# Six projection groups of a decoder step multiplied in plain fp32 from raw weights, with their norm scaling on VectorE

## The chip, the cores and the metric

The kernel runs on one NeuronCore of one Trainium2 chip. The metric is the device time of one execution in microseconds, the median of several runs. Engines are named TensorE (PE in the profile), VectorE (DVE), ScalarE (ACT), GpSimd (POOL) and SyncE (SP, which here only issues transfers).

## The reference

One layer of a decoder, for a prompt of 256 tokens and 8 decode tokens, everything in float32:

```
x = x + 0.5 * post1(SwiGLU_1(pre1(x)))
h = rms_norm(x, g_pre) @ w_in             # 2048 -> 5120: q, k, v of 8 window heads and of 4 stick-breaking heads, q of 4 memory heads
q, k of the window heads are rotated (rope)
o = [dilated window attention | stick-breaking attention | memory attention]
x = x + post(concat(rms_norm of each part of o) @ w_out)
x = x + 0.5 * post2(SwiGLU_2(pre2(x)))
```

The 264 tokens go through the dense parts together. The prompt attends to itself and to a memory of 256 rows; each decode token attends to its cache: 2048 positions of stick-breaking keys in pages of 128, the window keys and 256 memory rows. The new keys and values are outputs too.

## The kernel before

Activations lie transposed in SBUF: 16 tiles of 128 features by 264 tokens (xT). Every dense layer runs over weight **chunks** of 1 MB (4 x 128 rows by 512 columns), loaded by SyncE into four slots `raw`. A chunk is two **units**. For a unit ScalarE rounds the weights to a high half (`wh<-raw`, L780), VectorE subtracts that for the low half (`wl<-raw,wh`, L1111), and TensorE makes three products of a reduced fp32 type for each tile: high x high, high x low and low x high (L471 to L473, in `unit`). The activations have such halves too, xh and xl. The splits run three units ahead of the products (`AHEAD`), and semaphores count them: `hi_made`, `lo_made`, `unit_used`.

The input projection (L578 to L602) has ten groups of 512 columns, each four chunks. Groups 0 to 3 give the queries: VectorE takes them from PSUM with the norm factor r_pre (`take_projection`). Groups 4 to 9 give keys and values: ScalarE copies them into kv (`take_kv`, L896), GpSimd makes the low halves of their weights (L1657) and multiplies kv by r_pre (`scale_kv`, L1664).

While groups 5 to 9 run, VectorE goes through the decode **sequences** (`sequence`, L1295, two hardware loops of four with the rotation of the new keys between them). A sequence has 12 key tiles: 8 of paged keys, 3 of window keys, 1 of memory keys. For each tile VectorE makes 8 dot products of the keys with the query rows (L1305, k_cache). SyncE's queue holds the order of the loads (L409 to L423): for each sequence its query rows, its 12 key tiles into four slots, each as the slot is freed (`k_used`), and behind every fourth tile the next weight chunk. k_cache lies over xT, which is parked in DRAM for that time.

The queries must first leave TensorE: after group 4 it turns them (L597), ScalarE copies them (q_s, L912), GpSimd stores them to q_scratch, and SyncE loads them back onto all partitions (q_rows, L388).

When all 24 tiles of kv are scaled (`kv_scaled`), TensorE turns them into 18 rows of 512 (L615, L617). ScalarE copies them out, twelve of them through two alternating buffers `rows` (L931) that GpSimd's stores must free, six into v_rows. In ScalarE's order the scores of the decode tokens (zt, L951) come behind these rows, and they need the whole sequence loop. Then come the values of the caches, w_out and the second feed-forward part.

## Time and profile before

| | |
|---|---|
| runs of before | 2578.55, 2571.93, 2576.32 us; median 2576.32 |
| profiled execution | span 2581.1 us; no time of its own is listed beside it |
| PE busy | 2227.8 us, 86% of the span |
| DVE, ACT, POOL busy | 1546.8, 1016.3, 484.8 us |
| transfers | 468.32 MB, mean 181 GB/s |

Stages in the span, read from the chain in order of time: memory projection and first feed-forward part to about 905 us, input projection and sequence loop to 1368, attention to about 1612, output projection and second feed-forward part to the end. Busy shares are averages over stages with different limits, so a stage is read by its own stretch. A duration of a matmul in the trace reaches over its pipeline; the distance of two starts is what it costs in a row of them.

### The profile page before, as it was taken

Reading aid. Unit: us, or ns where it says so; the run is one execution under the profiler, and the core shown is the slowest. Engines: PE = TensorE matmul, PEld = TensorE weight load, DVE = VectorE, ACT = ScalarE, POOL = GpSimd, SP = SyncE. Lnnn points to the kernel's source line nnn. Section 1 sums busy time; section 2 is a strip of 40 time slices with the busy share of each in tenths; the row PEclk is TensorE's granted clock in tenths of the full one; section 3 lists DMA queues with packets and bytes.
Section 4 is the critical chain, followed back from the end, with each engine's and each line's share of the span. In section 5 each row is a group of like instructions: output and inputs, shape, how many; then the busy total and the mean of one; then the engine's idle time right before and its main releaser. Section 6 shows DMA issues by size and latency. Waiting matters only on the chain.

```text
span 2581.1 us, 44451 instructions
## 1 busy us (share of the span) xinstructions
PE 2227.8 (86%) x16613; PEld 2104.8 (82%) x16613; DVE 1546.8 (60%) x3309; ACT 1016.3 (39%) x1300; POOL 484.8 (19%) x444
## 2 busy tenths in 40 slices
PE   6899999999999879665545766888999999999997
PEld 6899999999999869655532323878999999999996
DVE  6655555554545574588787866546554555555456
ACT  3443343443434443211125775334443334343343
POOL 4600000000000242535331212035000000000004
PEclk9999999999999989877767988888999999999998
DMA  7355455554555537577786965343554545455451
GB/s 255 122 196 180 163 180 164 180 180 164 177 167 180 164 98 244 158 249 252 224 292 221 289 209 175 131 147 115 181 181 162 181 163 180 164 180 181 163 180 66
DMA packets 230311, 468.32 MB, mean 181 GB/s; under 512 B 12689, under 2 KB 13714, under 8 KB 229346
## 3 DMA queue, kind: packets, MB, share of 16 engines
q1 hardware_dynamic: 227602, 460.78, 54.3%
q0 software_dynamic: 2528, 4.89, 0.5%
q8 instruction: 144, 2.36, 0.4%
q14 instruction: 37, 0.30, 0.0%
HBM read 456.40 MB, written 9.21 MB: 180 GB/s over the span
## 4 chain that ended last, share of the span: by engine, by line
PE 70%; DVE 14%; DMA 5%; POOL 3%; ACT 3%; issue 3%; SPq 1%; DVEq 0%; ACTq 0%; POOLq 0%
PE ps L471 23%; PE ps L472 22%; PE ps L473 22%; DVE k_cache L1305 6%; DMA k_cache<-win_k 2%; DVE vl L1469 2%; DVE wl L1111 1%; POOL acc L1589 1%; DMA k_cache<-sb_k 1%; ACT wh L780 1%; POOL wl L1657 1%; ACT vh L1019 1%; DVE y L1173 1%; PE ps L702 1%; PE ps L704 1%
## 5 line engine op out<-in xcount | busy, mean ns | idle before, releaser
L471 PE MATMUL ps<-xh,wh 128*128 128x264 f32 (+1 forms) x3840 | 1136.8, 296 | 197.0 <-POOL wl L1657 106.5
L1111 DVE TENSOR_TENSOR wl<-raw,wh 128x1024 fp32r<-128x1024 f32 x605 | 749.9, 1243 | 814.6 <-ACT wh L780 813.5
L780 ACT ACTIVATE wh<-raw 128x1024 fp32r<-128x1024 f32 x656 | 690.2, 1058 | 1277.4 <-PE ps L473 1046.8
L472 PE MATMUL ps<-xl,wh 128*128 128x264 f32 (+1 forms) x3840 | 1127.5, 294 | 0.0
L473 PE MATMUL ps<-xh,wl 128*128 128x264 f32 (+1 forms) x3840 | 1125.6, 293 | 0.0
L471 PEld LDWEIGHTS ps<-xh,wh 128*128 128x128 f32 x3840 | 761.0, 198 | 213.5 <-POOL wl L1657 98.1
L472 PEld LDWEIGHTS ps<-xl,wh 128*128 128x128 f32 x3840 | 760.6, 198 | 0.0
L473 PEld LDWEIGHTS ps<-xh,wl 128*128 128x128 f32 x3840 | 758.1, 197 | 0.0
L471 PE MATMUL ps<-hh,wh 128*128 128x264 f32 x1408 | 400.6, 284 | 0.0
L473 PE MATMUL ps<-hh,wl 128*128 128x264 f32 x1408 | 400.5, 284 | 0.0
L472 PE MATMUL ps<-hl,wh 128*128 128x264 f32 x1408 | 400.3, 284 | 0.0
L1642 POOL TENSOR_TENSOR gate<-gate,r_pre 128x264 f32<-128x264 f32 x88 | 85.5, 1001 | 1330.8 <-ACT gate L837 1330.8
L1305 DVE CUSTOM_DVE_ANT_0 k_cache<-k_cache,q_rows 128x128 f32<-128x128 f32 (+1 forms) x768 | 228.5, 365 | 73.6 <-DMA k_cache<-win_k 42.4
L471 PEld LDWEIGHTS ps<-hh,wh 128*128 128x128 f32 x1408 | 265.6, 189 | 0.0
L472 PEld LDWEIGHTS ps<-hl,wh 128*128 128x128 f32 x1408 | 265.3, 188 | 0.0
L473 PEld LDWEIGHTS ps<-hh,wl 128*128 128x128 f32 x1408 | 264.7, 188 | 0.0
L1657 POOL TENSOR_TENSOR wl<-raw,wh 128x1024 fp32r<-128x1024 f32 x51 | 129.3, 2552 | 225.9 <-ACT wh L780 225.8
L1469 DVE TENSOR_TENSOR vl<-v_cache,vh 128x1024 fp32r<-128x1024 f32 (+1 forms) x96 | 116.3, 1240 | 50.4 <-ACT vh L1019 50.0
L702 PE MATMUL ps<-vh,weights 128*8 128x512 f32 (+1 forms) x192 | 86.4, 450 | 55.7 <-DVE vl L1469 54.8
L1204 DVE TENSOR_TENSOR y<-y,ps 128x264 f32<-128x264 f32 x352 | 127.4, 423 | 5.1 <-PE ps L473 5.0
L1019 ACT ACTIVATE vh<-v_cache 128x1024 fp32r<-128x1024 f32 (+1 forms) x96 | 98.7, 1049 | 28.6 <-PE ps L704 19.2
L702 PEld LDWEIGHTS ps<-vh,weights 128*8 128x8 f32 (+1 forms) x192 | 18.0, 94 | 110.7 <-DVE vl L1469 86.0
(215 smaller groups left out, 1247.1 us busy)
## 6 DMA issues: line engine op xcount, KB each, us to landing
raw<-w_gu SPq DMA_DIRECT2D x176, 1024.0 KB, 5.0
raw<-w_down SPq DMA_DIRECT2D x88, 1024.0 KB, 5.1
raw<-w_in SPq DMA_DIRECT2D x40, 1024.0 KB, 6.3
k_cache<-sb_k SPq DMA_DIRECT2D x128, 256.0 KB
v_cache<-sb_v SPq DMA_DIRECT2D x128, 256.0 KB, 3.6
raw<-w_out SPq DMA_DIRECT2D x16, 1024.0 KB, 5.2
raw<-w_mem_kv SPq DMA_DIRECT2D x8, 1024.0 KB, 10.2
k_cache<-win_k SPq DMA_DIRECT2D x16, 384.0 KB
```

The lines of the kernel that those rows point to most:

```text
L471: pe.matmul(out, w_hi, rh(k0 + kk), start=first and kk == 0, stop=False)
L472: pe.matmul(out, w_hi, rl(k0 + kk), start=False, stop=False)
L473: mm = pe.matmul(out, w_lo, rh(k0 + kk), start=False, stop=last and kk == 1)
L702: pe.matmul(out[0:8, :], weights[0:n, 2 * k + j, b], vh[slot][0:n, part], start=first, stop=False, skip_group_check=True)
L780: act.activation(wh[:, c % UNIT_SLOTS], raw[:, raw_slot, 2 * (c % 2):2 * (c % 2) + 2], ACT.Copy).then_inc(hi_made, 1)
L1019: act.activation(vh[slot][0:n], v_cache[0:n, tile % V_SLOTS], ACT.Copy).then_inc(vh_made, 1)
L1111: dve.tensor_tensor(wl[:, c % UNIT_SLOTS], raw[:, (c // 2) % RAW_SLOTS, part], wh[:, c % UNIT_SLOTS].bitcast(F32), ALU.subtract).then_inc( ...
L1204: dve.tensor_tensor(y[:, b], y[:, b], ps[4 * (q % 2) + j][:, 0:TOK], ALU.add).then_inc(y_added[l], 1)
L1305: return dve.tensor_tensor_reduce(keys, keys, q_rows[0:n, HD * q_head:HD * q_head + HD], 1.0, 0.0, ALU.mult, ALU.add, zb[0:n, col:col + 1])
L1469: dve.tensor_tensor(vl[slot][0:n], v_cache[0:n, tile % V_SLOTS], vh[slot][0:n].bitcast(F32), ALU.subtract).then_inc(vl_made, 1)
L1642: pool.tensor_tensor(gate[:, j], gate[:, j], r_pre[:], ALU.mult).then_inc(gate_ready[l], 1)
L1657: pool.tensor_tensor(wl[:, c % UNIT_SLOTS], raw[:, (c // 2) % RAW_SLOTS, part], wh[:, c % UNIT_SLOTS].bitcast(F32), ALU.subtract).then_inc ...
```

## The change

Groups 4 to 9 are multiplied in plain fp32: one product of the raw weights with xg, the activations times the norm's gain, where there were three of the halves (`plain_chunk`). ScalarE makes xg after group 3, over xh. No weights of these groups are split, so GpSimd has no arithmetic there, and the counts that later stages wait for are lowered by `SPLIT_SKIP` = 48 units. A chunk is loaded when the products of the chunk four before it are done. The queries are turned after two chunks of group 4. VectorE scales kv (`scale_kv`) at five places in the sequence loop, which is written out, and once behind it. SyncE loads the chunks 16 to 19 ahead of the first key tiles, and these wait for xg.

```diff
+SPLIT_SKIP = 2 * (CH_OUT - CH_PLAIN)
...
+def made(unit):
+    return unit if unit < 2 * CH_PLAIN else unit - SPLIT_SKIP
...
+            xg = sb("xg", [P, KT, TOK], F32, part)
...
+                if 20 <= n < 44:
+                    sp.wait_ge(unit_used, unit_of(CH_IN + n - 3))
+                    load_chunk(CH_IN + n, c, src, first=True)
+                else:
+                    load_chunk(CH_IN + n, c, src, skip=SPLIT_SKIP if n >= 44 else 0)
...
-            for n in range(12, 16):
+            for n in range(12, 20):
                 load_in(n)
             sp.wait_ge(x_parked, 16)
+            sp.wait_ge(xg_ready, KT)
             for k in range(K_SLOTS):
                 load_tile(0, k, k_cache[:, k], k_loaded[k], sb_k, win_k, mem_k)
-            for n in range(16, 16 + 6):
+            for n in range(20, 16 + 6):
                 load_in(n)
...
+            def plain_chunk(g, c, guard=None):
+                n, bank = CH_IN + 4 * g + c, 4 * (g % 2)
+                pe.wait_ge(w_loaded[c], 16 * (n // RAW_SLOTS + 1))
+                for j in range(4):
+                    if c == 0:
+                        pe.wait_ge(in_read, (g - 2) * 4 + (j + 1))
+                    if guard is not None:
+                        guard(j)
+                    for kk in range(4):
+                        k = 4 * c + kk
+                        if g == 4 and j == 0:
+                            pe.wait_ge(xg_ready, k + 1)
+                        mm = pe.matmul(ps[bank + j][:, 0:TOK], raw[:, c, kk, P * j:P * j + P], xg[:, k],
+                                       start=k == 0, stop=k == KT - 1)
+                    if c == 3 and j < 3:
+                        mm.then_inc(in_done, 1)
+                mm.then_inc(unit_used, 2)
...
-            for c in range(8, 32):
+            for c in range(8, 32 - AHEAD):
                 split(u_in + c + AHEAD)
+            act.wait_ge(unit_used, u_in + 32)
+            for k in range(KT):
+                act.activation(xg[:, k], xT[:, k], ACT.Copy, scale=G[:, G_PREM + k:G_PREM + k + 1]
+                               ).then_inc(xg_ready, 1)
...
+            def scale_kv(g):
+                at = 4 * (g - 4)
+                for j in range(4):
+                    dve.wait_ge(in_read, 4 * g + j + 1)
+                    dve.tensor_tensor(kv[:, at + j], kv[:, at + j], r_pre[:], ALU.mult).then_inc(kv_scaled, 1)
...
+                    g, after = divmod(b * TILES_B + k + 38, 16)
+                    if after == 0 and 4 <= g < 9:
+                        scale_kv(g)
...
-            with dve.Fori(0, DEC // 2) as b:
+            for b in range(DEC // 2):
                 sequence(b)
             dve.wait_ge(kv_scaled, H_WIN)
             rope(kv[:, 0:H_WIN])
-            with dve.Fori(DEC // 2, DEC) as b:
+            for b in range(DEC // 2, DEC):
                 sequence(b)
+            scale_kv(9)
```

TensorE's order around the turning of the queries (qT), which before stands between groups 4 and 5:

```order
L473 MATMUL ps<-xh,wl 128x264
L597 MATMUL ps<-ident,qT 8x128 [waits in_read,roped]
L597 MATMUL ps<-ident,qT 8x128 x15
L471 MATMUL ps<-xh,wh 128x264 [waits q_s_made,lo_made]
L472 MATMUL ps<-xl,wh 128x264
```

The same place of the changed kernel:

```order
L625 MATMUL ps<-xg,raw 128x264 [waits xg_ready,w_loaded1]
L625 MATMUL ps<-xg,raw 128x264 [waits xg_ready] x3
L625 MATMUL ps<-xg,raw 128x264 x12
L637 MATMUL ps<-ident,qT 8x128 [waits in_read,roped]
L637 MATMUL ps<-ident,qT 8x128 x15
L625 MATMUL ps<-xg,raw 128x264 [waits xg_ready,w_loaded2]
```

The turning now follows the chunk in slot 1, half of group 4, and the next products do not wait for q_s_made.

GpSimd's order before, from the low halves (wl) to the store of the queries:

```order
L1657 TENSOR_TENSOR wl<-raw,wh 128x1024 [waits hi_made,lo_made]
L1657 TENSOR_TENSOR wl<-raw,wh 128x1024 [waits hi_made] x10
L1664 TENSOR_TENSOR kv<-kv,r_pre 128x264 [waits in_read] x4
L1602 DMA q_scratch<-q_s 8x2048 [waits q_s_made]
L1657 TENSOR_TENSOR wl<-raw,wh 128x1024 [waits hi_made] x8
```

The same place now:

```order
L1643 TENSOR_TENSOR acc<-acc,sq 128x264 [waits squared_mix,sq_made_mix] x6
L1656 DMA q_scratch<-q_s 8x2048 [waits q_s_made]
L1656 DMA out<-rows 128x512 [waits kv_rows_made] x2
L1656 DMA out<-rows 8x512 [waits kv_rows_made]
```

Between the query store and the stores of the key rows GpSimd has nothing left.

VectorE's order at the end of the last sequence, now:

```order
L1376 COPY zw<-zb 128x24
L1378 COPY zm<-zb 128x8
L1342 TENSOR_TENSOR kv<-kv,r_pre 128x264 [waits in_read,z_kept]
L1342 TENSOR_TENSOR kv<-kv,r_pre 128x264 [waits in_read] x3
L1392 COPY small<-kv 128x64 [waits roped,kv_scaled]
```

The four scalings of group 9 stand behind the last sequence; before, GpSimd had made them on its own.

## Rows read from the trace of the kernel before

**Rows 1.** The page: span, and its chain of waits by line.
```profile
span 2581.1 us, 44451 instructions
PE ps L471 23%; PE ps L472 22%; PE ps L473 22%; DVE k_cache L1305 6%; DMA k_cache<-win_k 2%; DVE vl L1469 2%; DVE wl L1111 1%; POOL acc L1589 1%; DMA k_cache<-sb_k 1%; ACT wh L780 1%; POOL wl L1657 1%; ACT vh L1019 1%; DVE y L1173 1%; PE ps L702 1%; PE ps L704 1%
```

**Rows 2.** The chain in order of time: start us, us, what.
```profile
1052.09 2.80 POOL kv L1664 x4
1054.89 2.78 DMA q_scratch<-q_s
1057.69 5.06 DMA q_rows<-q_scratch
```

**Rows 3.** Timeline of VectorE, TensorE, ScalarE, 1024 to 1051: start, us, instruction.
```profile
1024.23 0.43 DVE L1264 TENSOR_TENSOR qT<-ps,r_pre 128x264 f32<-128x264 f32 x1 [0.29 <-PE ps L473]
1024.76 1.26 DVE L1279 COPY swap<-qT 64x2112 f32<-64x2112 f32 x1
...
1048.14 1.91 PE L597 MATMUL ps<-ident,qT 128*8 128x128 f32 x16
1048.78 2.02 ACT L912 ACTIVATE q_s<-ps 8x512 f32<-8x512 f32 x4
```

**Rows 4.** Line L1305 (ns min/median/max), then timeline of VectorE and GpSimd.
```profile
L1305 DVE CUSTOM_DVE_ANT_0 k_cache<-k_cache,q_rows x768: 276/281/2530, 1062.9 to 1366.4; 128x128 f32<-128x128 f32 x160, 96x128 f32<-96x128 f32 x32
...
1066.54 2.43 DVE L1305 CUSTOM_DVE_ANT_0 k_cache<-k_cache,q_rows 128x128 f32<-128x128 f32 x1
...
1068.90 2.44 DVE L1305 CUSTOM_DVE_ANT_0 k_cache<-k_cache,q_rows 128x128 f32<-128x128 f32 x1
...
1066.47 4.72 POOL L1657 TENSOR_TENSOR wl<-raw,wh 128x1024 fp32r<-128x1024 f32 x2 [8.60 <-ACT wh L780]
```

**Rows 5.** The dots' group on the page; their busy time in the last sequence.
```profile
L1305 DVE CUSTOM_DVE_ANT_0 k_cache<-k_cache,q_rows 128x128 f32<-128x128 f32 (+1 forms) x768 | 228.5, 365 | 73.6 <-DMA k_cache<-win_k 42.4
...
1338.80:1366.60 27.80, 20.95 (x96) 0.50 0.98 355
```

**Rows 6.** Windows: length, busy PE, PEld, DVE, ACT, POOL, clock, DMA share, GB/s.
```profile
1057.70:1357.90 300.20, 163.21 (x970) 153.58 (x968) 241.88 (x1498) 54.02 (x76) 123.22 (x76) 0.72 0.79 256
1400.00:1496.00 96.00, 77.34 (x308) 31.29 (x308) 81.94 (x134) 73.45 (x99) 20.83 (x30) 0.95 0.94 291
...
1338.80:1366.60 27.80, 11.03 (x44) 7.00 (x44) 21.01 (x191) 7.70 (x15) 7.98 (x15) 0.50 0.98 355
...
1331.00:1361.00 30.00, 16.27 (x72) 11.35 (x72) 23.09 (x208) 9.96 (x18) 9.42 (x18) 0.56 0.93 332
```

**Rows 7.** Groups of VectorE by shape: count, busy us, mean ns.
```profile
L1188 DVE TENSOR_TENSOR hl<-hidden,hh 128x264 fp32r<-128x264 f32 x88 | 37.8, 429 | 6.7 <-ACT hh L843 4.0
...
L1285 DVE TENSOR_TENSOR kv<-kv,swap 128x2112 f32<-128x2112 f32 x1 | 2.8, 2782 | 0.0
```

**Rows 8.** Timeline of TensorE at two places.
```profile
1127.35 0.42 PE L471 MATMUL ps<-xh,wh 128*128 128x264 f32 x1
...
1128.01 0.42 PE L471 MATMUL ps<-xh,wh 128*128 128x264 f32 x1
...
1570.65 0.59 PE L663 MATMUL ps<-spent,ones 128*128 128x256 f32 x2
...
1571.08 0.60 PE L664 MATMUL ps<-spent,tri 128*128 128x256 f32 x2
```

**Rows 9.** Group of ScalarE by shape.
```profile
L789 ACT ACTIVATE xh<-xT,G 128x264 fp32r<-128x264 f32 x48 | 22.8, 507 | 10.8 <-POOL xT L1596 10.8
```

**Rows 10.** ScalarE's timeline at the key rows; landing of the tile rows.
```profile
1332.56 0.60 ACT L931 ACTIVATE rows<-ps 128x512 f32<-128x512 f32 x1 [5.50 <-PE ps L615]
...
1360.24 0.59 ACT L931 ACTIVATE rows<-ps 8x512 f32<-8x512 f32 x1 [2.28 <-DMA out<-rows]
1368.08 1.75 ACT L951 ACTIVATE zt<-zsb,bias 128x128 f32<-128x128 f32 x4 [7.25 <-DVE small L1342]
...
DMA to landing us min/median/max: 2.8/4.1/5.9
```

**Rows 11.** Waits of SyncE's queue, 1000 to 1370: total, times, longest.
```profile
SPq L375 <- DVE zb L1305: 124.8, 21, 20.3
```

More of the change, by code:

```diff
@@ L145, in decoder_step @@
             xl = sb("xl", [P, KT, TOK], F32R, part)
+        with ExitStack() as part:
+            xg = sb("xg", [P, KT, TOK], F32, part)
         with ExitStack() as part:
@@ L308, in load_const, with load_chunk @@
                 sp.dma_start(tile, src).then_inc(const_loaded, 16)
-            def load_chunk(n, slot, src, first=False):
+            def load_chunk(n, slot, src, first=False, skip=0):
                 if not first:
-                    sp.wait_ge(lo_made, 2 * n - 6)
+                    sp.wait_ge(lo_made, 2 * n - (6 + skip))
                 sp.dma_start(raw[:, slot], src).then_inc(w_loaded[slot], 16)
@@ L460, in _, with unit @@
         def _(pe):
-            def unit(v, slot, rh, rl, k0, bank, width, first, last, done=None, guard=None):
-                pe.wait_ge(lo_made, v + 1)
+            def unit(v, slot, rh, rl, k0, bank, width, first, last, done=None, guard=None, skip=0):
+                pe.wait_ge(lo_made, v + (1 - skip))
                 for j in range(4):
@@ L476, in unit, with group @@
                 mm.then_inc(unit_used, 1)
-            def group(v, width, bank, done, guard, ready=None):
+            def group(v, width, bank, done, guard, ready=None, skip=0):
                 for c in range(8):
@@ L558, in ffn @@
                 pe.wait_ge(rooted, nth(name))
[L559 removed]
+                group(u0 + 8, TOK, 4, u_done[l], guard_u, skip=skip)
                 with pe.Fori(0, (FF_STEPS - 1) // 2) as pair:
@@ L589, in _ @@
             in_group(1, 1, lambda j: wait_one(j, rooted, nth("mix")))
-            for g in range(2, 5):
+            for g in range(2, 4):
                 in_group(g, g % 2)
+            def plain_chunk(g, c, guard=None):
[15 more added lines that the diff above has]
+                mm.then_inc(unit_used, 2)
+            plain_chunk(4, 0)
+            plain_chunk(4, 1)
             pe.wait_ge(roped, 1)
@@ L598, in _ @@
                 mm.then_inc(q_turned, 1)
-            in_group(5, 1, lambda j: pe.wait_ge(q_s_made, j + 1))
-            with pe.Fori(0, 2) as pair:
-                for a in range(2):
-                    in_group(pair * 2 + (6 + a), a)
+            plain_chunk(4, 2)
+            plain_chunk(4, 3)
+            plain_chunk(5, 0, lambda j: pe.wait_ge(q_s_made, j + 1))
+            for c in range(1, 4):
+                plain_chunk(5, c)
+            for g in range(6, 10):
+                for c in range(4):
+                    plain_chunk(g, c)
             pe.wait_ge(roped, 2)
@@ L743, in guard @@
                         pe.wait_ge(out_read, 4 * (g - 2) + j + 1)
-                group(u_out + 8 * g, TOK, 4 * ((g + 1) % 2), out_done, guard, xl_ready["out"] if g == 0 else None)
+                group(u_out + 8 * g, TOK, 4 * ((g + 1) % 2), out_done, guard, xl_ready["out"] if g == 0 else None,
+                      SPLIT_SKIP)
             pe.wait_ge(out_read, 16)
@@ L904, in take_kv @@
                                    ps[4 * par + j][:, 0:TOK], ACT.Copy).then_inc(in_read, 1)
-            for c in range(32, 40):
-                split(u_in + c + AHEAD)
-            act.wait_ge(in_read, 16)
-            take_kv(4, 0)
             for b in range(4):
@@ L912, in _ @@
                 act.activation(q_s[:, 512 * b:512 * b + 512], ps[4 + b][0:DEC, :], ACT.Copy).then_inc(q_s_made, 1)
-            for c in range(40, 48):
-                split(u_in + c + AHEAD)
-            take_kv(5, 1)
-            with act.Fori(0, 2) as pair:
-                for a in range(2):
-                    for c in range(8):
-                        split(u_in + 48 + 8 * a + c + AHEAD, pair, 16)
-                    take_kv(pair * 2 + (6 + a), a)
+            act.wait_ge(in_read, 16)
+            for g in range(4, 10):
+                take_kv(g, g % 2)
+            for c in range(AHEAD):
+                split(u_in + 80 + c)
             used = 0
@@ L1108, in split @@
                         return
-                dve.wait_ge(hi_made, i * per + (c + 1))
+                dve.wait_ge(hi_made, i * per + (made(c) + 1))
                 part = slice(2 * (c % 2), 2 * (c % 2) + 2)
@@ L1347, in _ @@
                               ALU.max).then_inc(top_part, 1)
+            for c in range(AHEAD):
+                split(u_in + 80 + c)
             dve.wait_ge(s_soft, 1)
@@ L1648, in _ @@
             update("mix", "post1")
-            u_in = unit_of(CH_IN)
-            def split(c, i=0):
-                pool.wait_ge(hi_made, i * 16 + (c + 1))
-                part = slice(2 * (c % 2), 2 * (c % 2) + 2)
-                pool.tensor_tensor(wl[:, c % UNIT_SLOTS], raw[:, (c // 2) % RAW_SLOTS, part],
-                                   wh[:, c % UNIT_SLOTS].bitcast(F32), ALU.subtract).then_inc(lo_made, 1)
-            def scale_kv(g, block):
-                for j in range(4):
-                    pool.wait_ge(in_read, g * 4 + (j + 1))
-                    x = kv[:, bass.ds(block + j, 1)].rearrange("p a t -> p (a t)")
-                    pool.tensor_tensor(x, x, r_pre[:], ALU.mult).then_inc(kv_scaled, 1)
-            pool.wait_ge(lo_made, u_in + 32)
-            for c in range(AHEAD):
-                split(u_in + 32 + c)
-            for c in range(8):
-                split(u_in + 32 + AHEAD + c)
-            scale_kv(4, 0)
             pool.wait_ge(q_s_made, 4)
             store(q_scratch, q_s[:], q_stored)
-            for c in range(8):
-                split(u_in + 40 + AHEAD + c)
-            scale_kv(5, 4)
-            with pool.Fori(0, 2) as pair:
-                for a in range(2):
-                    for c in range(8):
-                        split(u_in + 48 + 8 * a + c + AHEAD, pair)
-                    scale_kv(pair * 2 + (6 + a), pair * 8 + (8 + 4 * a))
             used = 0
```

27 lines of the change are left out of this document (14 added, 13 removed).

## The prediction

> **What bounds the kernel now.** I read the page's totals and its chain of waits first [rows 1]: over the span TensorE has 70% of the chain, but VectorE's key dot products (L1305) have 6% and the loads of window keys 2%, and those are not spread over the span. In order of time the chain leaves TensorE at 1024 us, goes through GpSimd's low halves (wl, L1657) and its scaling of kv, then through the two small transfers that bring the decode queries back [rows 2], and stays with the dot products and their loads until 1366. So the change lies in one stretch, 1024 to 1368 us, in which TensorE is not the limit; outside it the instructions are the same but for wait counts.
>
> Inside it I distinguish three pieces. (1) From the end of projection group 3 (its last take starts at 1024.23) to the first dot product at 1062.9 [rows 3, 4]. (2) The sequence loop, 1062.9 to the last dot product's end at 1366.6, 303.7 us. (3) From there to the first scaling of scores on ScalarE at 1368.08 [rows 10], 1.5 us.
>
> The loop is VectorE's with waits for keys. 768 dot products take 228.5 us and 73.6 us are waits, 20.0 of them before the loop [rows 5]. They are not all alike: the median is 0.28 us and the longest 2.53; a dot product that meets a GpSimd subtract lasts as long as that subtract: at 1066.54 and 1068.90 two take 2.43 and 2.44 us, while GpSimd runs two of 4.72 us together [rows 4]. In the last sequence, where GpSimd does no arithmetic, 96 take 20.95 us, 0.218 each [rows 5]. At that pace 768 are 167.6 us: 61 us of the 228.5 is GpSimd's doing. But the 16 DMA engines are 0.79 busy over the loop and 0.98 in the last sequence [rows 6], so the next limit is close, and SyncE's queue mostly waits for the dot products to free a key slot (124.8 us in one line alone [rows 11]): faster dots will issue loads sooner and meet that limit.
>
> **Start of the loop.** Removed ahead of the query transposes: half of group 4, the splits of its weights, and GpSimd's 2.80 us of scaling that stands ahead of the query store [rows 2]. Added: 16 scalings into xg on ScalarE, which cannot start before group 3 is done since xg lies over xh; the like operation is 22.8 us for 48, 0.475 each [rows 9], so 7.6 us from 1024.3, to 1032. TensorE follows four tiles behind it: a plain fp32 product shows as two records; two pairs of 256 columns start 0.43 us apart (1570.65, 1571.08) at the full clock [rows 8], so 264 columns are 0.443 us and a chunk of 16 products 7.1 us. The first block of chunk 0 is paced by ScalarE (2.4 us instead of 1.8). Two chunks: 1024.3 + 0.6 + 7.1 + 7.1 = 1039. The rotation of the queries, which they also need, is over by then: it starts at 1024.76, and its five parts without GpSimd beside them are some 11 us. From transposes to the copied queries it is 2.7 us (1048.14 to 1050.80 [rows 3]): 1041.7. Then the store lands after 2.78, the rows after 5.06 + 0.18 [rows 2]: 1049.7. Against it: the first four key tiles now wait for xg on SyncE and are issued at 1032 with two weight chunks, some 4 MB that are still landing when the small store goes out; I add 1.3 us. Query load at 1046, first dot product at 1051, 11.9 us earlier (ends 6 and 14).
>
> **The loop.** VectorE's own sum: 167.6, plus 20 in-loop scalings of kv by a like subtract of 37.8/88 = 0.43 us [rows 7], 8.6, plus 8 ends of a sequence at 1.2, plus the key rotation, about 11 (its last part is 2.78 us [rows 7]): 197 us. TensorE: 22 chunks of 7.1 us, 156. Transfers: the same packets as now, 0.79 x 300.2 = 237 us of all 16 engines [rows 6], less the row stores that leave the loop (3.2 MB; 332 GB/s at a share of 0.93 is 357, so 9 us), plus 2 for the last tile: 230 us. That is the longest sum. No stretch keeps the engines full: 0.94 in the value stage, whose loads are also bound by slots, 0.98 in the last sequence [rows 6]. I take 0.94: 245 us, plus 5 for the first query rows and the last tile's use, 250 from the query load at 1046, thus to 1296, against 1366.6. Counted from the first dot product: 245 against 303.7, 58.7 us less. Ends: 0.98 and a second less at the seams, 235; a share of 0.85, since only four key slots stand between the two, 275. Covered, hence nothing: VectorE's scalings (a pause of 1.7 us while three tiles are in flight), ScalarE's takes, the loop's branches. SyncE's order is the same, but a weight chunk n now waits until chunk n-4 is multiplied, not split, and the key tiles behind it in the queue wait too. A chunk is issued every four tiles, about 10 us; chunk n-4 was issued 40 us before and needs 8 to landing and 7 to 14 of TensorE. No wait, except for the first, chunk 18, some 3 us while the first queries land.
>
> **After the loop.** The last scaling, group 9, stands behind the last sequence, and TensorE's 18 row turns wait for all 24. Now those rows run under the last sequence, for nothing: ScalarE's first copy is at 1332.56, its last ends at 1360.83, 28.3 us, because two row buffers alternate with stores that land in 2.8 to 5.9 us, median 4.1 [rows 10]. ScalarE's score work stands behind them. So all of it becomes visible: 1.8 us of scaling, an estimated 1.1 for the turns to the first copy, then the copies. The other traffic is less there (six value tiles, 3.1 MB, then none). With every store at 2.8 and 0.9 from a copy's start to its store it would be under 6 rounds of 3.7 us, 21; as now 28; I take 22.7: 25.6 us to ScalarE's scores instead of 1.5, 24.1 later (ends 22 and 30). The three splits for w_out that VectorE gets stand beside this.
>
> From the scores on everything is as before, shifted. Sum: -11.9 - 58.7 + 24.1 = -46.5 us. The profiled execution has no time of its own listed apart; its span of 2581.1 [rows 1] is 4.8 above the median of the runs, so 2534.6 in such a profile and 2530 as the median.
>
> **The Trainium skill on two points.** The share and rate of the last sequence are 0.98 and 355 GB/s [rows 6]. The Trainium skill, SBUF — State Buffer, section "A bandwidth-pool intuition that's wrong", gives 358 GB/s for HBM to one core. By that alone the loop's 75.5 MB (92 key tiles 46.1, query rows 8.4, 20 chunks 21.0) would be 211 us and the loop 34 us shorter than my 245; the trace has 256 GB/s over the loop at a share of 0.79, 324 when full, since query rows and window keys move slower per byte. I go by the engines' time.
>
> **Rivals.** (a) TensorE becomes the loop's limit. Its granted clock is 0.72 of full over the loop, with idle time between chunks [rows 6], and at 1126 to 1128 three products are 0.66 us, 0.22 each: 1.2 GHz [rows 8]. If plain products stayed at that level a chunk is 32 records x 0.44 = 14.1 us; chunk 37 ends at 1041 + 20 x 14.1 = 1323, SyncE holds the last chunk and 16 key tiles behind it, 27 us of dots: end 1350, scores at 1376 instead of 1368, 8 us slower: 2584. It decides from 13.7 us per chunk. Against it: at 14.1 TensorE would be busy without a break, and in the value stage, busy for 77 of 96 us, it has a clock of 0.95 [rows 6], nearly all at 2.4 GHz. The Trainium skill, TensorE: Matmul & The Clock Gate, section "HAM oscillation", says that waits between bursts of matmuls put it back to the low clock each time; the trace agrees for the starts of bursts, and by that rule a chunk would be 9 to 10 us and still hidden. (b) Transfers go faster than I think and VectorE's 197 us is the end: loop 205, 40 us less, 2490. Against it the share of 0.98 already reached at the slower pace. (c) Four slots starve both, or stalls of the dots have another source: loop 280, 2565. Against it the match of lengths in [rows 4]. (d) The row turns don't hide less because stores are quick: 15 us instead of 24, inside my range.
>
> **Numbers.** Forecast 0.79; (a), (b) and (c) 0.07 each. The forecast's ends: loop 235 to 275, start and tail 6 together: 2508 to 2562; the lower end goes to 2503 to take in part of (b). About 0.3%, 8 us, is what can be told from no change. Faster 0.79 + 0.07 + 0.04 of (c) = 0.90; within 0.3% 0.03 of (c) and 0.02 of (a), 0.05; slower the other 0.05 of (a).
>
> **What would show it.** Dot products all near 0.22 us, with a total near 168; first one near 1051; DMA share above 0.9 from there; waits of dots for keys still some 50 us; loop end near 1296; then 18 rows in about 24 us with VectorE idle; plain chunks of 7 to 10 us; xg 7.6 us. Wrong if long dots remain without GpSimd, if SyncE waits for TensorE in mid-loop, or if the share stays near 0.8.

## The result, and the profile after

Four timed runs of the changed kernel have a median of 2532.01 us (2528.70 to 2539.06), four of the kernel before, timed beside them, 2575.52 us (2571.93 to 2578.55). The ratio is 0.9835, 95% interval 0.9818 to 0.9852: 1.65% faster. The forecast was 2530.

| us | before | after | forecast |
|---|---|---|---|
| profiled execution / its span | none apart / 2581.1 | 2530.98 / 2528.9 | 2534.6 in such a profile |
| first dot product starts | 1062.9 | 1052.3 | 1051 |
| last dot product ends | 1366.6 | 1302.8 | 1296 |
| ScalarE's first scores (zt) | 1368.1 | 1324.9 | 1321.6 |
| from there to the end of the span | 1213.0 | 1204.0 | unchanged |

The last line is read first, since it limits what spans can tell. No instruction behind the scores was changed, yet this part is 9 us shorter in this profile. In the twelve experiments below it took 1204.0 to 1212.1 us. The clock that was granted to TensorE goes with it: from 240 to 300 us behind the first scores, as the output projection starts, the windows (columns as in [rows 6]) are, before and after,

```profile
1608.10:1668.10 60.00, 49.77 (x336) 47.97 (x337) 35.91 (x57) 22.23 (x36) 2.97 (x3) 0.83 0.38 127
...
1564.90:1624.90 60.00, 49.99 (x364) 48.57 (x363) 36.93 (x54) 22.80 (x36) 4.04 (x3) 0.90 0.39 133
```

Over all fourteen profiles it goes together: before, query rows once, light chunks and scaling on GpSimd have 0.83 to 0.84 there and 1210.8 to 1213.0 us behind the scores, the ten others 0.89 to 0.90 and 1204.0 to 1208.4. Why a kernel gets the one clock or the other no run here shows. So I compare places inside the stretch up to the scores, which repeat within a microsecond or two, and take a total as no finer than about 8 us.

The page of the profile after, the groups of the dot products and of the plain products (line, engine, operation, tiles, shape, count | busy us, mean ns | waits before it); the first answers to [rows 5]:

```profile
L625 PE MATMUL ps<-xg,raw 128*128 128x264 f32 x768 | 184.1, 403 | 41.6 <-DMA raw<-w_in 40.9
L1354 DVE CUSTOM_DVE_ANT_0 k_cache<-k_cache,q_rows 128x128 f32<-128x128 f32 (+1 forms) x768 | 165.6, 284 | 84.4 <-DMA k_cache<-win_k 50.6
```

The 768 dot products cost 165.6 us of busy time where they cost 228.5; the waits grew from 73.6 to 84.4, of which 20.0 and 18.6 lie ahead of the loop. One line's instances of it (ns min/median/max, first and last start), against [rows 4]:

```profile
L1354 DVE CUSTOM_DVE_ANT_0 k_cache<-k_cache,q_rows x768: 278/283/294, 1052.3 to 1302.5; 128x128 f32<-128x128 f32 x160, 96x128 f32<-96x128 f32 x32
```

The longest was 2530 ns and is 294 ns: no dot product is long any more. The windows (start:end, length, busy PE, PEld, DVE, ACT, POOL with counts, clock, DMA share, GB/s), against [rows 6]:

```profile
1052.30:1302.70 250.40, 157.48 (x651) 129.12 (x649) 184.21 (x1582) 11.64 (x25) 0.00 (x0) 0.85 0.94 306
1275.40:1302.80 27.40, 0.00 (x0) 0.00 (x0) 23.01 (x206) 0.00 (x0) 0.00 (x0) 0.50 0.95 293
1303.00:1325.00 22.00, 15.71 (x74) 12.20 (x74) 5.81 (x13) 10.19 (x19) 8.98 (x17) 0.60 0.48 177
```

Over the loop the transfers went from a share of 0.80 at 261 GB/s (the loop's own stretch before, whose row stands further below) to 0.94 at 306; VectorE is busy for 184 of 250 us, TensorE for 157. The second row is the last sequence: 293 GB/s at a share of 0.95, where the kernel before had 355 at 0.98, so a like share is not a like rate. The third row is new: 22 us in which VectorE is nearly idle and the DMA engines half.

The chain of waits of the profile after (start, us, what), its start and its place behind the loop, against [rows 2] and [rows 10]:

```profile
1024.12 14.48 PE ps L625 x64
1038.60 0.45 PE ps L637 x4
1039.07 2.02 ACT q_s L957 x4
1041.38 5.97 DMA q_scratch<-q_s
...
1303.53 1.12 DVE kv L1342 x3
1304.79 1.10 PE ps L659 x4
1305.91 0.61 ACT rows L973
1306.52 0.28 issue
1306.80 2.34 DMA out<-rows
```

Two chunks are 14.48 us, the query store lands after 5.97 (it was 2.78). Behind the loop stand the last scaling, the turns, and then copy and store by turns.

### The profile page after: what moved, and what is told of

It is laid out like the page before. It is cut to its first block, busy times and chain, and to the rows that moved or that the text cites. A ratio compares the mean times of both kernels' runs of the same rounds, so it can differ in the third digit from the quotient of the medians.

```text
span 2528.9 us, 43387 instructions
## 1 busy us (share of the span) xinstructions
PE 2223.6 (88%) x16229; PEld 2074.6 (82%) x16229; DVE 1477.8 (58%) x3336; ACT 976.1 (39%) x1268; POOL 330.8 (13%) x369
## 4 chain that ended last, share of the span: by engine, by line
PE 72%; DVE 10%; DMA 7%; ACT 4%; issue 4%; POOL 3%; SPq 1%; POOLq 0%; ACTq 0%; DVEq 0%
PE ps L489 23%; PE ps L490 23%; PE ps L491 23%; DMA k_cache<-win_k 3%; DVE k_cache L1354 3%; DMA k_cache<-sb_k 2%; DVE vl L1524 1%; DVE wl L1153 1%; POOL acc L1643 1%; ACT wh L825 1%; ACT vh L1061 1%; PE ps L746 1%; DVE xl L1165 1%; PE ps L748 1%; POOL acc L1630 1%
## 5 line engine op out<-in xcount | busy, mean ns | idle before, releaser
L489 PE MATMUL ps<-xh,wh 128*128 128x264 f32 (+1 forms) x3456 | 1005.0, 291 | 89.6 <-issue 38.6
L825 ACT ACTIVATE wh<-raw 128x1024 fp32r<-128x1024 f32 x608 | 640.8, 1058 | 1029.7 <-PE ps L491 1019.5
L490 PE MATMUL ps<-xl,wh 128*128 128x264 f32 (+1 forms) x3456 | 999.6, 289 | 0.0
L491 PE MATMUL ps<-xh,wl 128*128 128x264 f32 (+1 forms) x3456 | 998.3, 289 | 0.0
L489 PEld LDWEIGHTS ps<-xh,wh 128*128 128x128 f32 x3456 | 670.1, 194 | 100.5 <-issue 49.7
L490 PEld LDWEIGHTS ps<-xl,wh 128*128 128x128 f32 x3456 | 669.2, 194 | 0.0
L491 PEld LDWEIGHTS ps<-xh,wl 128*128 128x128 f32 x3456 | 667.3, 193 | 0.0
L625 PE MATMUL ps<-xg,raw 128*128 128x264 f32 x768 | 184.1, 403 | 41.6 <-DMA raw<-w_in 40.9
L1354 DVE CUSTOM_DVE_ANT_0 k_cache<-k_cache,q_rows 128x128 f32<-128x128 f32 (+1 forms) x768 | 165.6, 284 | 84.4 <-DMA k_cache<-win_k 50.6
L625 PEld LDWEIGHTS ps<-xg,raw 128*128 128x128 f32 x768 | 151.7, 199 | 73.5 <-DMA raw<-w_in 45.5
```

The costliest lines, as they stand in the source:

```text
L489: pe.matmul(out, w_hi, rh(k0 + kk), start=first and kk == 0, stop=False)
L490: pe.matmul(out, w_hi, rl(k0 + kk), start=False, stop=False)
L491: mm = pe.matmul(out, w_lo, rh(k0 + kk), start=False, stop=last and kk == 1)
L625: mm = pe.matmul(ps[bank + j][:, 0:TOK], raw[:, c, kk, P * j:P * j + P], xg[:, k], start=k == 0, stop=k == KT - 1)
L825: act.activation(wh[:, c % UNIT_SLOTS], raw[:, raw_slot, 2 * (c % 2):2 * (c % 2) + 2], ACT.Copy).then_inc(hi_made, 1)
L1354: return dve.tensor_tensor_reduce(keys, keys, q_rows[0:n, HD * q_head:HD * q_head + HD], 1.0, 0.0, ALU.mult, ALU.add, zb[0:n, col:col + 1])
```

## The experiments

My theory had four parts: GpSimd's subtracts made the dot products long; with them gone, the transfers set the loop; TensorE keeps out of the way unless a chunk takes much longer; the row stage is exposed only by the place of the last scaling. "First scores" below is ScalarE's first zt; "loop" is from the first dot product's start to the last one's end. All times of places are from profiles. The experiments ran on three chips, each beside the kernel before; its medians there were 2579.79, 2575.77 and 2578.22 us, so totals are compared by their ratios to it where a ratio was timed.

| kernel | first dot | loop | last dot to first scores | first scores | timed, us (runs) |
|---|---|---|---|---|---|
| before | 1062.9 | 303.7 | 1.5 | 1368.1 | 2575.52 (4) |
| changed | 1052.3 | 250.5 | 22.1 | 1324.9 | 2532.01 (4) |
| subtracts put back | 1052.3 | 297.0 | 21.3 | 1370.6 | 2578.84 (1) |
| half of the dots | 1053.7 | 236.3 | 23.4 | 1313.4 | 2522.49 (1) |
| query rows once | 1052.5 | 226.1 | 22.8 | 1301.4 | 2514.16 (1) |
| light chunks | 1051.0 | 231.5 | 22.3 | 1304.8 | 2518.10 (1) |
| query rows four tiles earlier | 1051.4 | 240.7 | 22.5 | 1314.6 | 2523.43 (1) |
| products twice | 1062.1 | 320.6 | 21.8 | 1404.5 | 2614.22 (1) |
| queries turned later | 1063.9 | 253.0 | 22.1 | 1339.0 | 2548.55 (1) |
| scaling on GpSimd | 1052.4 | 256.4 | 0.9 | 1309.7 | 2520.15 (4) |
| the same, looped | 1052.2 | 255.1 | 1.3 | 1308.6 | 2518.76 (1) |
| scalings inside the loop | 1054.0 | 250.0 | 5.5 | 1309.5 | 2517.09 (4) |
| the same, earlier | 1052.7 | 250.2 | 0.9 | 1303.8 | 2516.90 (5) |
| both (below) | 1052.3 | 241.1 | 1.0 | 1294.3 | 2504.95 (5) |

### What made the dot products long

Forty subtracts are put back on GpSimd, with results that nobody uses. The cuts of the code below leave out other places with "...", here the new semaphore's.

```diff
...
+            act.wait_ge(pool_runs, 40)
             for c in range(AHEAD):
                 split(u_in + 80 + c)
...
+            for i in range(40):
+                pool.wait_ge(unit_used, unit_of(CH_IN) + 37 + i)
+                if i >= 4:
+                    pool.wait_ge(pool_runs, i - 3)
+                pool.tensor_tensor(wl[:, i % UNIT_SLOTS], wh[:, (i + 1) % UNIT_SLOTS].bitcast(F32),
+                                   wh[:, i % UNIT_SLOTS].bitcast(F32), ALU.subtract).then_inc(pool_runs, 1)
```

> The changed kernel with 40 subtracts of 128x1024 on GpSimd put back into the loop (two per weight chunk, results used by nobody, started as TensorE uses up each chunk), the rest unchanged. Theory (a GpSimd subtract holds the dot products that meet it for about 2.4 us each, two of them per subtract, since 4.72 us of GpSimd go with two long dots): some 60 to 80 dot products of over 2 us appear, L1354's total goes from 218 us (768 x 0.284) or what its rows give to about 60 us or more above the changed kernel's, the loop from 250 to 285 to 310 us, total 2565 to 2590 us. Rival (the long dot products came from the split's other parts or from key rows that were late, not from GpSimd): no dots over 0.6 us, loop within 4 us of 250, total within 4 us of 2531.

Measured: the groups of the page of this run, and a place of its timeline.

```profile
L1712 POOL TENSOR_TENSOR wl<-wh 128x1024 fp32r<-128x1024 f32 x40 | 98.9, 2492 | 141.5 <-PE ps L625 141.5
...
1085.84 2.38 POOL L1712 TENSOR_TENSOR wl<-wh 128x1024 fp32r<-128x1024 f32 x1
1085.95 2.42 DVE L1355 CUSTOM_DVE_ANT_0 k_cache<-k_cache,q_rows 128x128 f32<-128x128 f32 x1
...
1052.30:1349.20 296.90, 177.89 (x652) 141.88 (x650) 251.79 (x1582) 11.66 (x25) 94.45 (x39) 0.78 0.81 258
```

The dot that starts 0.11 us behind a subtract lasts 2.42 us, the subtract 2.38. (The Trainium skill, SBUF — State Buffer, "SBUF: two separate sides", says that VectorE with two SBUF inputs and GpSimd take one pair of ports by turns, each for a whole instruction; this row agrees.) Nothing reads these subtracts' results, so only their running can matter. By length, 29 dots of this run last over 2 us, 70.2 us together; the kernel before has 24 such (57.7 us) and 16 more of 0.6 to 2 us, the changed kernel none over 0.3. I had expected 60 to 80, two for each subtract: a subtract holds up less than one. The dots' busy time is 227.0 us (before 228.5, changed 165.6), the loop 297.0 us (before 303.7), the DMA share falls back to 0.81 (before 0.80 over the same stretch). The rival is out: by one run, 46.5 of the 53.2 us that the loop gained are GpSimd's subtracts. The forecast's assumed size (61 us of 228.5) is 61.4 here.

### What sets the loop now

Every second dot product left out, for paged, window and memory keys alike:

```diff
-                            for h in range(H_SB):
+                            for h in range(0, H_SB, 2):
...
```

> Every second of the 768 key dot products is left out; the loads, the scalings and the products of TensorE stay. If the transfers bound the loop (DMA share 0.87 to 0.95 over it, and 84.4 us of waits ahead of the dots), the 83 to 109 us of VectorE work that goes turns into waits: the loop is 235 to 245 us instead of 250, total 2518 to 2528. If VectorE's own work and the waits it causes by freeing key slots late is the limit, the loop falls with it, by 60 to 80 us, total 2450 to 2470.

```profile
1053.70:1290.00 236.30, 157.86 (x652) 129.18 (x650) 107.76 (x814) 11.55 (x25) 0.00 (x0) 0.86 0.98 321
```

VectorE's work fell by 76 us and the loop by 14: the transfers at a share of 0.98 are the rest, as the first case of the expectation had it. So 236 us is what this set of transfers takes, and VectorE still costs 14 us on top.

The query rows loaded for one sequence of eight:

```diff
-                        load_queries(b, H_WIN, H_SB, q_loaded[0])
+                        if b == 0:
+                            load_queries(b, H_WIN, H_SB, q_loaded[0])
...
```

> The decode queries' rows, each one row of scratch written to all 128 partitions, are loaded for the first of the eight sequences alone (7 of 8 left out, 7.3 MB of 75 MB of what lands in the loop; the other sequences use the first one's queries). With transfers as the limit and these rows priced by their bytes at the loop's 304 GB/s the loop is 24 us shorter, total 2507. If such rows are slower per byte than other loads, as the forecast took it from 324 GB/s when full against 355 in the last sequence, more: 35 to 60 us, total 2471 to 2496. If the transfers are not the limit: under 8 us.

The loop is 226.1 us, 24.4 less: about their bytes at the loop's mean rate, and without them share and rate stay what they were, 0.94 and 305 GB/s. They are not dearer per byte than the mean. That the total was 2514 and not 2507 lies behind the scores, which came 23.6 us earlier. The dots' waits in this run:

```profile
DVE k_cache L1356 <- DMA k_cache<-win_k: 26.7, 8, 6.6
DVE k_cache L1356 <- DMA q_rows<-q_scratch: 18.7, 1, 18.7
DVE k_cache L1356 <- DMA k_cache<-sb_k: 14.6, 11, 2.7
```

All 24 us come out of the wait for window keys (50.6 in the changed kernel); the wait for far keys (sb_k, 14.8) did not move. That does not look like an even shortage of bytes. A quarter of the bytes for 18 weight chunks asks the same from the other side:

```diff
+                if 22 <= n < 40:
...
+                    sp.dma_start(raw[:, c, 0:1], src[:, 0:1]).then_inc(w_loaded[c], 16)
```

> 18 of the weight chunks that are loaded inside the sequence loop bring a quarter of their bytes (256 KB instead of 1 MB each, 14.2 MB less; three quarters of their products then use old weights); key tiles, query rows, dot products and TensorE's products stay. If the transfers bound the loop at a mean of 304 GB/s, 14.2 MB are 46 us, but VectorE's own work stands below that at about 197 us plus the seams where no key is there; half the dots left out gave 236 us and 7.3 MB of query rows less gave 226, so I expect 205 to 220 us instead of 250, total about 2495 to 2505. If what the dot products wait for is not the amount of transfers but the order in which SyncE gives them out (window keys late behind the query rows), then under 10 us: total above 2520.

This expectation failed: twice the bytes of the query rows are gone and the loop is 231.5 us, 19.0 less instead of 30 to 45, with the share down to 0.89:

```profile
1051.00:1282.40 231.40, 156.86 (x659) 129.49 (x657) 184.12 (x1582) 12.06 (x26) 0.00 (x0) 0.85 0.89 272
```

41.4 us of waits for window keys stay. One reason lies in the price that I gave these bytes. I had taken 46 us from the mean rate, but share times length of the loop fell from 235 to 206 us: some 29 us for 14.2 MB of chunks, where 7.3 MB of query rows were 23 (estimates from the windows' shares). The other 10 us became idle time of the transfers, and there the amount of bytes is not the whole: SyncE gives out 768 KB of query rows for the memory and window heads right ahead of the window keys, and with four key slots VectorE runs dry there. Put four tiles earlier:

```diff
-                    if k == PAGES // 2:
+                    if k == 4:
                         sp.wait_ge(k_used, b * TILES_B + TILES_B)
                         load_queries(b, H_WIN + H_SB, H_MEM, q_loaded[1])
```

> SyncE gives out the query rows of the memory and window heads (768 KB) at key tile 4 of each sequence instead of right ahead of its window keys. The waits for window keys, 50.6 us in the changed kernel, 5 to 11 us in each sequence, follow these rows in the queue, and without the rows of seven sequences they were 26.7. If the order makes these waits (window keys late behind 768 KB that nobody needs yet), they fall to about 25 us and the loop to 236 to 242 us, total 2518 to 2523. If the amount does (transfers at a share of 0.94 over the whole loop), the wait only goes over to the far keys (sb_k up from 14.8 by some 20 us) and the loop stays within 3 us of 250, total within 4 us of 2531. I hold the second for somewhat likelier.

```profile
DVE k_cache L1354 <- DMA k_cache<-sb_k: 28.1, 14, 3.9
DVE k_cache L1354 <- DMA k_cache<-win_k: 26.9, 8, 6.0
...
1051.40:1292.00 240.60, 155.52 (x651) 127.19 (x649) 184.35 (x1582) 11.65 (x25) 0.00 (x0) 0.86 0.96 315
```

I had held the other case for likelier; the loop came out as in the first (236 to 242 us), the total just above it. For the waits the truth is between: 23.7 us of window waits go, 13.3 come back as waits for far keys, and the loop is 9.8 us shorter at a share of 0.96. Order was worth some 10 of the 14 us that stood between the loop and the 236 us of the transfers.

### Where TensorE would decide

Each plain product is issued twice:

```diff
...
+                        for twice in range(2):
+                            mm = pe.matmul(ps[bank + j][:, 0:TOK], raw[:, c, kk, P * j:P * j + P], xg[:, k],
+                                           start=k == 0 and twice == 0, stop=k == KT - 1 and twice == 1)
```

> Each plain product of the projection is issued twice (the sums come out doubled in groups 4 to 9), so a chunk is 14.5 us at the full clock, the 14.1 us of rival (a) at the low one; nothing else changes. By the forecast's account of that rival TensorE then sets the loop: chunk 37 ends at 1025 + 22 x 14.5 + 3 = 1347, SyncE holds the last weight chunks and 16 key tiles behind it, 27 to 35 us: the last dot product at 1374 to 1382 instead of 1303, total 2602 to 2612. If instead TensorE has room for it (the transfers are late anyway, and chunks wait for them 41 us in the loop), the loop's end moves by the 14.5 us of the start alone: total 2545 to 2550.

```profile
1055.00:1380.00 325.00, 313.46 (x1410) 267.35 (x1408) 181.50 (x1557) 13.12 (x29) 0.57 (x1) 0.99 0.71 239
```

With chunks of twice the length TensorE is the loop: busy for 313 of 325 us, last dot product's end at 1382.7 (expected 1374 to 1382), total 2614.22, 2 us above the range. Rival (a)'s mechanism is real. Its price was put too low, and my expectation came out by two errors against each other: chunk 37 was done at 1340.0 (a chunk every 14.24 us) and not 1347, and the last dot product ended 42.7 us behind it, not the 27 that the forecast has or the 27 to 35 that I expected. With 42.7 in the forecast's own sum, rival (a) ends at 1366 and not 1350. The low clock, its cause, did not come: kept busy, TensorE has 0.99 of the full clock. In the changed kernel, where it pauses for chunks, a single chunk takes 7.4 to 9.3 us and one with another right behind it up to 9.8 (timeline of TensorE, with the pause before it in brackets; x64 are two chunks, the second of 7.1):

```profile
1111.48 16.68 PE L625 MATMUL ps<-xg,raw 128*128 128x264 f32 x64 [7.06 <-DMA raw<-w_in]
1131.36 7.39 PE L625 MATMUL ps<-xg,raw 128*128 128x264 f32 x32 [3.19 <-DMA raw<-w_in]
1143.24 9.05 PE L625 MATMUL ps<-xg,raw 128*128 128x264 f32 x32 [4.50 <-DMA raw<-w_in]
...
1200.84 9.26 PE L625 MATMUL ps<-xg,raw 128*128 128x264 f32 x32 [8.10 <-DMA raw<-w_in]
...
1212.44 7.39 PE L625 MATMUL ps<-xg,raw 128*128 128x264 f32 x32 [2.34 <-DMA raw<-w_in]
...
1231.16 9.08 PE L625 MATMUL ps<-xg,raw 128*128 128x264 f32 x32 [1.88 <-DMA raw<-w_in]
```

Of the eleven bursts of this loop that follow a wait for a chunk, five began slowly: the four behind the longest pauses (4.50, 5.88, 7.06 and 8.10 us) and one behind 1.88. The six others, behind 1.41 to 3.19 us, took 7.39. The pause alone does not say which. The forecast's 13.7 us was the chunk at which the change would gain nothing. TensorE sets the loop's end earlier: with the 42.7 us above, 1041 + 20 chunks + 42.7 reaches the measured end of 1302.8 at 11 us a chunk (an estimate). The longest here, 9.8, is below that.

### What the start hangs on

The query transposes behind all four chunks of group 4:

```diff
+            plain_chunk(4, 2)
+            plain_chunk(4, 3)
             pe.wait_ge(roped, 1)
...
-            plain_chunk(4, 2)
-            plain_chunk(4, 3)
```

> The transposes of the decode queries stand behind all four chunks of group 4 on TensorE instead of behind two (the placement of before). Theory: the start of the loop hangs on the chain xg, chunks, transposes, store, rows, and a chunk is 7.24 us, so the first dot product comes 14.5 us later, at 1066 to 1067; the key tiles and chunks are in their slots by then, so the loop gives back a little of it (up to 5 us, the store lands in less traffic, 2.8 instead of 6.0); total 9 to 14 us more, 2540 to 2545. Rival: the store's landing and the rows wait for the key tiles' traffic in any case, so the start moves by less than 5 us and the total by less than 4.

```profile
1024.57 28.72 PE ps L625 x128
...
1056.07 2.79 DMA q_scratch<-q_s
1058.88 4.91 DMA q_rows<-q_scratch
```

The first dot product came 11.6 us later (expected 14.5): 14.2 for two chunks, 0.4 as group 3 ended later, less 3.2 because the store landed after 2.79 instead of 5.97 us. The chain is as forecast, and the store's 6 us go with the traffic at its time. The give-back inside the loop did not come (253.0 us, 2.5 more). First scores 14.1 us later; the total of 2548.55 is 3.6 above my range, less than what the part behind the scores varies by.

### The row stage and the scaling

The scalings of kv at earlier key tiles, none behind the loop:

```diff
-                    g, after = divmod(b * TILES_B + k + 38, 16)
-                    if after == 0 and 4 <= g < 9:
+                    g = {26: 4, 42: 5, 58: 6, 70: 7, 78: 8, 82: 9}.get(b * TILES_B + k)
+                    if g is not None:
                         scale_kv(g)
...
-            scale_kv(9)
```

> The kv scalings are given to VectorE at earlier key tiles (groups 4 to 9 at tiles 26, 42, 58, 70, 78, 82 instead of 26, 42, 58, 74, 90 and behind the loop), so that the 18 row turns, their copies and stores can run under the last sequence again. My theory, that the row stage behind the loop costs the 20.7 us that the two traces show (22.2 us from the last dot product to ScalarE's first scores, where it was 1.5) and that the place of the last scaling is what puts it there: the first scores come 1.5 to 8 us behind the last dot product, the loop itself gets up to 9 us longer since 3.2 MB of row stores move into it, total 12 to 19 us less than the changed kernel, 2513 to 2520 us. Rival: the row stores take the key loads' place in full and the value loads were waiting for the same engines anyway, so that only the order changes: gain under 4 us, 2528 to 2532.

The chain of this run behind the last scaling:

```profile
1274.95 1.39 DVE kv L1342 x4
1276.48 1.10 PE ps L659 x4
1277.60 0.61 ACT rows L973
...
1279.35 4.38 DMA out<-rows
1283.81 0.61 ACT rows L973
...
1284.70 4.59 DMA out<-rows
1289.37 0.59 ACT rows L973
...
1290.25 5.45 DMA out<-rows
```

From the last scaling to the first scores it is 34.6 us instead of 21.8, since the stores of this chain land after 4.4 to 5.9 us instead of 1.8 to 2.3, but it starts 28 us earlier. It ends 5.5 us behind the last dot product, and the loop is not longer (250.0). Timed ratio to before 0.9758, interval 0.9723 to 0.9792, against the changed kernel's 0.9835. The rival (nothing gained) is out.

The scaling back on GpSimd, each as soon as it can be:

```diff
...
+            for i in range(24):
+                pool.wait_ge(in_read, 17 + i)
+                pool.tensor_tensor(kv[:, i], kv[:, i], r_pre[:], ALU.mult).then_inc(kv_scaled, 1)
```

> The norm scaling of the 24 key and value tiles is given back to GpSimd, each as soon as ScalarE has copied it out (the part of the change that moved it to VectorE is undone, and with it the place of the last four behind the last sequence). A scaling on GpSimd took 0.70 us before, and a dot product that meets one lasts as long: 24 of them lengthen the dots by 7 to 17 us in sum, of which the waits for transfers take up most. The rows are turned as soon as group 9 is out, near 1257, and their copies and stores run under the last two sequences. My theory: loop 250 to 258 us, the row stage behind it 1.5 to 5 us instead of 22; total 10 to 18 us less than the changed kernel, 2513 to 2521. Rival (scaling is better on VectorE, as it leaves the dot products alone): the dots' 17 us come out in full and the loop ends past 1320, total 2528 to 2535.

```profile
L1698 POOL TENSOR_TENSOR kv<-kv,r_pre x24: 740/782/884, 1049.4 to 1257.7; 128x264 f32<-128x264 f32 x24
```

The dots' busy time is 177.0 us, 11.4 more, the loop 5.9 longer, and the row stage is hidden: first scores 15.2 us earlier than in the changed kernel; ratio 0.9771 (0.9732 to 0.9810). So this part of the change, as it was placed, cost about 15 us of what the others gained. VectorE was the better engine by 6 us in the loop (250.5 us, or 250.0 with the rows inside it too, against 256.4); the place behind the loop was the mistake.

VectorE's sequences as hardware loops again, on top of that:

```diff
-            for b in range(DEC // 2):
+            with dve.Fori(0, DEC // 2) as b:
                 sequence(b)
...
-            for b in range(DEC // 2, DEC):
+            with dve.Fori(DEC // 2, DEC) as b:
```

> The kernel with the scalings on GpSimd, with VectorE's sequences as two hardware loops of four again instead of written out (the part of the change that wrote them out is undone as well). The forecast put nothing on it: the loop's end costs a branch per sequence, VectorE waits for keys at that place anyway. Theory: loop within 2 us of the 256.3 us of the written-out one, total within 4 us of 2520 to 2524. Rival (each turn of the loop costs VectorE a microsecond or more that no slack takes up): 6 to 16 us more, 2527 or above.

Loop 255.1 against 256.4, total 2518.76: writing the sequences out is worth nothing by itself, as far as one run tells. It is needed only to put scalings at single tiles.

### The better version

The scalings inside the loop, the last three groups earlier still:

```diff
-                    g = {26: 4, 42: 5, 58: 6, 70: 7, 78: 8, 82: 9}.get(b * TILES_B + k)
+                    g = {26: 4, 42: 5, 58: 6, 68: 7, 74: 8, 79: 9}.get(b * TILES_B + k)
```

> As the kernel with the scalings inside the loop, but groups 7, 8 and 9 still earlier, at key tiles 68, 74 and 79 (group 9's last copy is out at 1256.3 us, tile 79 comes near 1262). With the scalings at tile 82 the rows' chain started at 1276.5 and its last copy ended at 1309.6, 5.6 us behind the last dot product; started some 12 us earlier it ends before the dot products do. The first scores then come 1.5 us behind the last dot product, 4 us earlier than there: 2509 to 2514 us, ratio to before 0.973 to 0.976. Rival (the row stores are slowed by the key loads as much as they are moved up, and slow the key loads in turn): same as that kernel, 2514 to 2518, or ratio 0.976.

The places came nearly as expected (first scores 0.9 us behind the last dot product, 5.7 us earlier than with tile 82; profiled execution 2510.36), the times did not: median 2516.9 (2510.36 to 2524.20), where I had 2509 to 2514 and the rival 2514 to 2518, ratio 0.9775 (0.9753 to 0.9797). Its interval and that of the version with tile 82 (0.9758) overlap, so it is not shown that these 5 us reach the end. With the query rows given out at tile 4 as well (the edit `k == PAGES // 2` to `k == 4` above):

> The kernel with scalings at tiles 26, 42, 58, 68, 74, 79, and the query rows of memory and window heads given out at tile 4. If the order of transfers matters, 8 to 14 us less than that kernel alone, 2497 to 2504 us; if only their amount does, the same within 3 us, 2508 to 2515.

```profile
1052.30:1293.30 241.00, 175.16 (x723) 141.31 (x721) 185.54 (x1585) 21.64 (x43) 9.64 (x18) 0.86 0.98 324
```

Median 2504.95 us (2500.44 to 2518.18), 12 us below the version before it, as the first case of the expectation had it within a microsecond; ratio 0.9734, interval 0.9708 to 0.9760, which just overlaps that version's (0.9753 to 0.9797), while the first scores are 9.5 us earlier. It is about 1% below the changed kernel (0.9818 to 0.9852), 2.7% below the kernel before. First scores at 1294.3, 30.6 us earlier than in the changed kernel. The share of the transfers over the loop is 0.98: as long as the bytes are the same, little more is to be had from their order.

## Why the prediction was right

**Start of the loop**, forecast -11.9 us, measured -10.6. The store was given out 0.3 us earlier than forecast (1041.38 instead of 1041.7), the rows took 0.3 less, and the store landed after 5.97 us where the sum had 2.78 and 1.3 for traffic. That was the real miss, 1.9 us. In the later run with the queries behind all of group 4, when key tiles and chunks had landed, it took 2.79.

**The loop**, forecast 245 us, measured 250.5. Dot products 167.6 forecast, 165.6 measured. VectorE's own sum was put at 197 us and is 184. The share of 0.94 that I took from the value stage is the one measured, and that is in part luck: it is no property of these loads, since the query rows four tiles earlier gave 0.96 and the last version 0.98. What was off is the term "transfers": 0.94 x 250.4 is 235 us of all 16 engines, where I had 230. I had read it from a window that ended 9 us before the loop did and added 2 us for the rest; the loop's own stretch in the profile of before has

```profile
1062.90:1366.60 303.70, 159.18 (x936) 149.76 (x936) 248.71 (x1561) 54.67 (x77) 124.55 (x77) 0.71 0.80 261
```

0.80 x 303.7 = 243, less 9 for the row stores 234. I also explained the low rate wrongly, by query rows being slower per byte: without them the loop lost only 24.4 us, their share at the mean rate. Whether window keys are slower no run shows.

**The bandwidth rule.** The forecast set the rule of 358 GB/s for one core (the Trainium skill, SBUF — State Buffer, "A bandwidth-pool intuition that's wrong") against the trace and went by the trace. Over a whole loop no kernel here moved more than 324 GB/s, at a share of 0.98, though in single slices of 6 us the changed kernel reached 387, above the figure; by the rule alone the forecast would have been 39 us short of the measured loop.

**SyncE's feared wait** for a used chunk: waits of its queue from 1040 to 1303 us (total, times, longest), against [rows 11]:

```profile
SPq L392 <- DVE zb L1354: 75.3, 19, 9.6
SPq L325 <- PE ps L625: 0.3, 1, 0.3
```

0.3 us where 3 were allowed; the wait for freed key slots fell from 124.8 to 75.3.

**After the loop**, forecast 25.6 us to the first scores, measured 22.1 (so +20.7 for +24.1). In the chain above the first row store lands after 2.34 us, quicker than the 2.8 I took as the quickest, at a DMA share of 0.48.

**The sum** at the first scores: -10.6 - 53.2 + 20.7 = -43.1 us, forecast -46.5; the timed medians differ by 43.5. The total of 2532.01 is 2 us from the forecast's 2530, nearer than its parts: the gain of start and loop was put 6.8 us too high, the loss behind the loop 3.4 too high. These misses cancel in part, and so far the closeness is luck. Of the loop's gain 46.5 us are the subtracts (their run), so about 7 us are left for the other parts. Most of that is GpSimd's too: its scalings of kv, put back alone, made the loop 5.9 us longer.

**Two slips in the sums.** The ends of the range do not come out of their terms: a loop of 235 to 275 us and 6 us for start and tail give 2514 to 2566, not 2508 to 2562. And the 275 takes a share of 0.85 with the 5 us counted from the query load; from the first dot product, as the 235 is, it is 271. The measured 2532 lies inside all of these.

**The rivals.** (b) VectorE as the end is out (184 of 250 us), (c) is out (no long dot is left, and the loop did not come near 280), though VectorE did still wait for late window keys, (d) was partly so: the stage was 3.5 us shorter than forecast. (a) stayed away because the plain products kept to 7.1 to 9.8 us a chunk. The forecast had cited "HAM oscillation" (the Trainium skill, TensorE: Matmul & The Clock Gate) for chunks of 9 to 10 us after a pause; of the eleven bursts after one, five agree nearly (9.05 to 9.8) and six do not (7.39).

## What to carry to other kernels

When an engine off the chain shares its time with one on it, look for instructions of the second whose length equals one of the first: the gain is at most the sum of those excesses (61 us here, of which 46.5 came out), up to the next limit, and the next limit is read from the DMA share. Give work that was moved to a busy engine a place by who waits for it, not by its own lateness: the last four scalings, 1.7 us of work, cost 15 to 21 us because a chain of small stores hung behind them. And where a queue hands out several kinds of loads in order, ask which of them nobody needs yet; a wait put down to one load may be made by the one ahead of it.

## What was not expected

The small query store (64 KB) lands after 2.8 us when key tiles and chunks have landed and after 6.0 among them; the row stores of 256 KB after a median of 2.3 us behind the loop and of 5.0 inside it (scalings at tile 82). A share of 0.94 did not mean that bytes alone were short: leaving out 7.3 MB saved 24.4 us of loop, leaving out 14.2 MB of other loads saved 19.0. Bytes differed in what they took of the engines' time (23 us against 29), and their place in the queue counted beside that. A scaling of 128x264 takes GpSimd 0.74 to 0.88 us and VectorE 0.42.
